# Blocks of 96 instead of 128 slots for the heavy experts of a mixture-of-experts stage on one Trainium2 core

## What is computed

```python
D_MODEL, SEQ, DEPTH = 1024, 1024, 2
N_EXPERTS, MOE_TOP_K, MOE_FF = 32, 2, 512
...
def _hier_moe(m, ...):                     # m: rmsnorm(h), 1024 tokens
    # one group of 8 experts per token, then its two best experts
    experts = g_idx * MOE_PER_GROUP + e_idx
    return _expert_dispatch(xf, experts, weights, w_gate, w_up, w_down)
...
    def expert_block(args):                # tok: the tokens of one expert e
        xb = x_pad[tok]
        hb = jax.nn.silu(xb @ w_gate[e]) * (xb @ w_up[e])
        return hb @ w_down[e]
```

## Time and profile before

| | us |
|---|---|
| median of 3 runs | 3237.29 |
| the 3 runs | 3237.29, 3222.32, 3237.57 |
| the profiled execution | 3239.65 |
| its span, first to last instruction | 3238.1 |
| mean granted TensorE clock | 0.945 of full |
| `first_blocks`, layer 0, first product to the start of the last | 852.7 to 1412.4 |
| `first_blocks`, layer 1, first product to the start of the last | 2489.7 to 3050.1 |

### The profile page before, as it was taken

One profiled execution on the slowest core, in us unless ns is written; L12 is line 12 of the kernel. 1 busy time (PEld: TensorE's weight loads), 2 busy tenths in 40 slices (PEclk: granted clock), 3 DMA queues, 4 the chain that ended last, 5 costly groups with the idle time before them and its releaser, 6 DMA issues. The chain is left out here.

```text
span 3238.1 us, 32792 instructions
## 1 busy us (share of the span) xinstructions
PE 2942.9 (91%) x12473; PEld 1583.8 (49%) x12474; DVE 1127.9 (35%) x2447; ACT 631.1 (19%) x1248; POOL 246.2 (8%) x352
## 2 busy tenths in 40 slices
PE   7999899999799999979799899577897999999798
PEld 5544555545444444434376644367654444444243
DVE  2584355544200000024371623566464000000052
ACT  3310355521100101112211111222211101101030
POOL 0000000001100000020000000134201000000110
PEclk9999899999799999989897799888997999999899
DMA  4000881031699999962110210000414999999641
GB/s 153 26 27 0 328 347 53 1 121 57 241 414 415 421 405 399 397 243 84 52 50 1 37 44 26 1 2 2 165 53 169 415 413 412 410 404 397 235 162 45
DMA packets 138550, 617.24 MB, mean 191 GB/s; under 512 B 25188, under 2 KB 31748, under 8 KB 121992
## 3 DMA queue, kind: packets, MB, share of 16 engines
q1 hardware_dynamic: 110952, 525.93, 41.2%
q0 software_dynamic: 24064, 86.00, 7.0%
q10 hardware_dynamic: 3376, 3.19, 0.3%
HBM read 508.00 MB, written 105.91 MB: 190 GB/s over the span
## 5 line engine op out<-in xcount | busy, mean ns | idle before, releaser
L1974 PE MATMUL acc<-wg,xt 128*128 128x512 f32 x512 | 222.9, 598 | 0.0
L737 PE MATMUL acc<-h,xt 128*128 128x512 f32 x384 | 165.2, 592 | 0.0
L2572 PE MATMUL acc<-xt,slabs 128*128 128x512 f32 x384 | 165.1, 592 | 0.0
L1974 PEld LDWEIGHTS acc<-wg,xt 128*128 128x128 f32 x512 | 98.5, 193 | 123.2 <-issue 123.2
L376 PE MATMUL scores<-qkt 65*128 65x512 f32 (+7 forms) x384 | 148.9, 498 | 0.9 <-DVE qkt L516 0.9
L522 DVE TENSOR_REDUCE nmax<-scores 128x1 f32<-128x256 f32 (+7 forms) x128 | 96.8, 756 | 77.5 <-PE scores L378 76.2
L1720 PE MATMUL py<-place 128*64 128x512 f32 (+1 forms) x352 | 120.2, 594 | 1.0 <-DVE place L1800 1.0
L1720 PE MATMUL pu<-place 128*128 128x512 f32 (+1 forms) x320 | 119.8, 593 | 0.0
L2572 PEld LDWEIGHTS acc<-xt,slabs 128*128 128x128 f32 x384 | 72.9, 190 | 91.4 <-issue 91.4
L737 PEld LDWEIGHTS acc<-h,xt 128*128 128x128 f32 x384 | 72.9, 190 | 91.1 <-issue 90.9
L1243 PE MATMUL acc<-place 128*128 128x512 f32 x256 | 114.3, 601 | 2.7 <-PEq L75 2.7
(11 more groups left out here) (645 smaller groups left out, 5170.1 us busy)
## 6 DMA issues: line engine op xcount, KB each, us to landing
own<-in_moe_w_gate_dram SPq DMA_DIRECT2D x22, 2048.0 KB, 16.3
place<-in_moe_w_down_dram SPq DMA_DIRECT2D x22, 2048.0 KB, 16.3
place<-in_moe_w_up_dram SPq DMA_DIRECT2D x20, 2048.0 KB, 18.2
slots_out<-zeros SPq DMA_DIRECT2D x4, 9216.0 KB, 62.8
place<-in_moe_w_gate_dram SPq DMA_DIRECT2D x18, 2048.0 KB, 21.2
own<-in_moe_w_up_dram SPq DMA_DIRECT2D x16, 2048.0 KB, 16.0
own<-in_moe_w_down_dram SPq DMA_DIRECT2D x10, 2048.0 KB, 19.5
xt<-in_moe_w_gate_dram SPq DMA_DIRECT2D x9, 2048.0 KB, 22.4
```

Source lines behind the costliest of these rows:

```text
L737: last = pe.matmul(acc[:, n % 4, 0:width], xs[:, k, tile_of(i)], weights[:, k, cols], start=(k == 0), stop=(k == k_of - 1))
L1974: last = pe.matmul(acc[:, u % 4, :], xt[:, k, i * P:(i + 1) * P], wg[:, k, n * SLAB:(n + 1) * SLAB], start=(k == 0), stop=(k == KD - 1))
L2572: last = pe.matmul(acc[:, n % 4, :], slabs[:, s % 2, k, (m % 4) * P:(m % 4 + 1) * P], xt[:, k, half * SLAB:(half + 1) * SLAB], start=(k == ...
```

## The change

The cap of a heavy expert is 96 in place of 128, in the rank table's column of caps as well. What a heavy unit moves, turns, copies and multiplies spans 96 slots: 96 rows of `xb` and `y`, 96 columns of each transpose's output, 96 stationary columns in each product. The ring, the order of the instructions, their number, the 512 moving columns of each product and the pairs are as before.

```diff
+ALONE, PAIRED = 96, 64
...
-    caps = [P if rank < HEAVY else P // 2 for rank in ranks]
+    caps = [ALONE if rank < HEAVY else PAIRED for rank in ranks]
...
-                    pool.dma_start(m[:, n, :], c.slots_in[units[n][0] * REGION:units[n][0] * REGION + P, :]).then_inc(c.x_in[n], 16)
+                    pool.dma_start(m[0:ALONE, n, :], c.slots_in[units[n][0] * REGION:units[n][0] * REGION + ALONE, :]).then_inc(c.x_in[n], 16)
...
+            def slots(n):
+                return ALONE if len(units[n]) == 1 else PAIRED
+
+            def used(n):
+                return slots(n) * len(units[n])
...
-                        last = pe.transpose(turned[:, k * P:(k + 1) * P], xb[:, n % 2].rearrange("t (p k) -> t k p", k=KD)[:, k, :], c.ident[:])
+                        last = pe.transpose(turned[:, k * P:k * P + used(n)], xb[0:used(n), n % 2].rearrange("t (p k) -> t k p", k=KD)[:, k, :], c.ident[0:used(n), 0:used(n)])
...
                 def product(n, kind, out, lhs, ks, k_last, cols):
-                    rows = P // len(units[n])
+                    rows = slots(n)
...
-                        last = pe.transpose(ph[:, k * P:(k + 1) * P], hid[:, k * P:(k + 1) * P], c.ident[:])
+                        last = pe.transpose(ph[:, k * P:k * P + used(n)], hid[0:used(n), k * P:(k + 1) * P], c.ident[0:used(n), 0:used(n)])
...
-                    act.activation(xbt[:, n % 2].rearrange("p k t -> p (k t)"), turned[:], ACT.Copy).then_inc(x_copied, 1)
+                    act.activation(xbt[:, n % 2, :, 0:used(n)], turned[:].rearrange("p (k t) -> p k t", k=KD)[:, :, 0:used(n)], ACT.Copy).then_inc(x_copied, 1)
...
-                    act.activation(y[:, n % 2, 0:SLAB], py[:, 0:SLAB], ACT.Copy).then_inc(y_act, 1)
+                    act.activation(y[0:used(n), n % 2, 0:SLAB], py[0:used(n), 0:SLAB], ACT.Copy).then_inc(y_act, 1)
...
-                    act.activation(gate, pg[:], ACT.Silu).then_inc(silued, 1)
+                    act.activation(gate[0:used(n)], pg[0:used(n)], ACT.Silu).then_inc(silued, 1)
...
-                    dve.tensor_copy(hidt.rearrange("p k t -> p (k t)"), ph[:]).then_inc(h_copied, 1)
+                    dve.tensor_copy(hidt[:, :, 0:used(n)], ph[:].rearrange("p (k t) -> p k t", k=KF)[:, :, 0:used(n)]).then_inc(h_copied, 1)
```

More of the change, by code:

```diff
@@ L1464, in _ @@
                 step(dve.tensor_scalar(cap_col[:], rank[:], float(HEAVY), None, ALU.is_lt))
-                step(dve.tensor_scalar(cap_col[:], cap_col[:], float(P // 2), float(P // 2), ALU.mult, ALU.add))
+                step(dve.tensor_scalar(cap_col[:], cap_col[:], float(ALONE - PAIRED), float(PAIRED), ALU.mult, ALU.add))
                 step(dve.tensor_tensor(over_col[:], counts, cap_col[:], ALU.subtract))
@@ L1671, in _ @@
                     if n >= RING:
-                        used, by, _ = tiles[n - RING]
-                        sp.wait_ge((gated, upped, downed)[used], (2 if used == 2 else 1) * (by + 1))
+                        before, by, _ = tiles[n - RING]
+                        sp.wait_ge((gated, upped, downed)[before], (2 if before == 2 else 1) * (by + 1))
                     sp.dma_start(ring[n % RING].rearrange("p (k n) -> p k n", k=KF if kind == 2 else KD),
@@ L1805, in y_half @@
                         dve.wait_ge(y_out[n % 2], y_before[n % 2] + 16 * arrivals[n - 2])
-                    dve.tensor_copy(y[:, n % 2, SLAB:D], py[:, SLAB:D]).then_inc(y_dve, 1)
+                    dve.tensor_copy(y[0:used(n), n % 2, SLAB:D], py[0:used(n), SLAB:D]).then_inc(y_dve, 1)
                 def results():
@@ L1838, in _ @@
                         dve.wait_ge(h_turned, n)
-                    dve.tensor_tensor(hid, gate, pu[:], ALU.mult).then_inc(hidden, 1)
+                    dve.tensor_tensor(hid[0:used(n)], gate[0:used(n)], pu[0:used(n)], ALU.mult).then_inc(hidden, 1)
                 hidden_out(UNITS - 1)
```

## The result

The changed kernel takes 3244.26 us (median of 22 runs, 3224.38 to 3249.72), the one before 3237.23 (22 runs, 3219.76 to 3239.58): a ratio of 1.0035 with a 95% interval of [1.002, 1.005]. It is 7 us slower by the medians, where 1 us faster was forecast. (The ratio says 11 us, since it is not that of the medians.) The time is inside the range given, by its upper end, but the sign is wrong, and not by chance, as the interval leaves out 1 and both layers show it. The profiled execution took 3246.25 us, with a span of 3244.7 and the same mean clock of 0.945.

What follows compares the result with a forecast made beforehand. TensorE was taken to bound the kernel, 20.6 of a heavy unit's 21.9 us being products. Terms 0 + 0 + 0.6 + 0.4 = 1.0 us less than the median 3237.29 gave 3236.3 us, range 3218 to 3246.

Steps and rivals of the forecast that it cites:

- Transfers: hidden before and after, 0: Heavy units' row loads and stores: 4.7 MB less a layer, asked for over a unit ahead, so no time gained.
- The weights wait for TensorE, not the reverse: Changed stage: TensorE has no wait for a DMA, while SP waits 168.5 us for up products to free ring tiles.
- Rival 2: DMA engines are the real bound in the stage; 9.4 MB less at 386 GB/s saves 24.4 us: 3212; chance 0.03.
- Transposes: 0, of 0 to 11.9 us: 432 transposes in heavy units keep 128 stationary columns, so 0.110 us each as before; gain 0 taken, 11.9 at most.
- Rival 1: Heavy units' transposes follow their moving columns, 128 to 96: 11.9 us more gained, 3224 us; chance 0.08.
- Products: 0.: Heavy units' products keep 512 moving columns, so 0.429 us a step with 96 stationary columns too: cost 0, gain 0.
- Rival 3: Array tiling changes at each transpose in heavy units, 0.6 us a unit, 22 us slower: 3258; chance 0.03.
- Rivals 4 and 5: 4: experts over 96 tokens bring overflow blocks, 3276, chance 0.01. 5: tiles still filled to 128, time as now.
- Loads laid bare beside a pair, -0.6: Stationary loads that cannot run ahead beside pairs: 0.075 for 0.10 us at 24 places, 0.6 us gained.
- copies, -0.4: ACT's copy falls to 0.81 us, on the path only at each stage's first gate: 0.2 us a layer, 0.4 gained.

Runs made afterwards that it cites:

- e2: The kernel before with only 96 rows of a heavy unit loaded and stored, compute still on 128 slots: 3243.83 us, ratio 1.0014 to before.
- s1: The changed kernel with 128 rows loaded, 96 stored, and only 2 of the 8 steps of every up product: 3221.21 us, one run.
- t1: As e4, but the 8 transposes `turned` take stationary columns that are neighbours in SBUF, with other results: 3224.86 us, one run.
- e1: The changed kernel with 128 rows of a heavy unit loaded and stored, compute on 96: 3228.42 us, ratio 0.9975 to before.
- s10: As s1, but the 128 rows of a heavy unit come in two loads of 96 and 32 rows: 3260.46 us, one run.
- e4: The changed kernel with 128 rows of a heavy unit loaded and 96 stored, compute on 96: 3229.63 us, ratio 0.9967 to before.

## Why the prediction was wrong

**"Transfers: hidden before and after, 0" is the step that failed.** It asked whether the rows of a unit arrive in time, and they do: TensorE never waited for them. It did not ask what their transfer does to the weights'. The term measures +5.8 / +6.2 us a stage, 12.0 us, in place of 0 (9.9 us by e2 against before), and its sign is the opposite of what 9.4 MB less suggest.

**The margin of the weights was misread.** "The weights wait for TensorE, not the reverse" was true of before, but it is a statement of sign and not of size. SP's waits only say that a ring tile was not free yet; they stayed at 161.5 us while the weights became late. The size of the margin was in sight: a DMA share of 1.01 in the earlier trace rows leaves little slack, and the demand, 401 GB/s of 408, works out from the earlier trace rows and the tiles' 2 MB, a margin of 2%. The earlier trace rows gave 386 GB/s in one window of 50 us, taken for what the engines do. One such window is too short for that: in s1, where TensorE waits for weights throughout, the same window has 374 GB/s and the whole stretch 407. From 900 to 1350 us before did 408.

**Rival 2, the DMA engines as the real bound, was right in its mechanism and wrong in its sign.** It was priced by bytes at a fixed rate, 24 us faster, chance 0.03. The rate was what changed. No rival had a smaller transfer that makes the others slower, though "transfers" was the one edit costed at nothing while its resource was full.

**Transposes: 0, of 0 to 11.9 us.** Between. `ph` follows its moving columns (0.083, the other end), 72 of them in a layer; `turned` hardly moves (0.107). The earlier trace rows showed that a full stationary load takes 0.106 where little moves; they do not bound a transpose of 96, as `ph` and t1's `turned` at 0.083 show. The gain is 0.13 us a unit, 2.3 us a stage, 4.6 in all. Rival 1 was right for a third of the transposes, and a term put at 0 was worth 4.6 us.

**Products: 0.** Right: 0.429 us a step with 96 stationary columns. **Rival 3**, a change of tiling: 21.80 us a unit in place of 22.5, so 96 columns count as 128 do. **Rivals 4 and 5** did not come about: no block over the cap, and rows of 96 in every form.

**Loads laid bare beside a pair, -0.6, and copies, -0.4.** Both about right. Three heavy units and a pair take 0.46 us less than before (22.57, 22.52, 22.04 and 21.93 us became 22.44, 22.46, 21.90 and 21.80), of which 0.39 are the transposes. That leaves 0.07 for the loads laid bare, where 0.05 was forecast. The copy took its 0.81 us, and the first gate's wait went from 1.11 us to 0.9.

The sum by the steps as measured: -5.7 for the narrower compute (e1 against before) and +12.0 for the transfers (after against e1) are +6.3 us. That they add up to the stages' difference is so by the way they are taken and proves nothing; e2 and before give +9.9 for the transfers on their own, and with it +4.2. The sign is the same, for 7.0 us between the medians. The prediction had named as its own test a stage off by over 5 us with unit periods as now, "for then I have missed what bounds its ends"; each stage is off by 3, with periods shorter than now, and what was missed does act at the end.

## What to carry to other kernels

"Engine X never waits" is not a margin. Where the DMA engines' share stands at 1, work out what the stage wants per second and what it gets, and follow the time from issue to landing along the stage: here a queue that shrinks (23.4, 16.2, 15.0 us) against one that doesn't (27.6, 31.1, 29.8) shows the loss by 1250 us, over 100 us before TensorE first waits for a tile. Beside heavy traffic, a smaller load may not be a cheaper one: cut the compute to what is in use, store what is in use, and keep row loads at 128 rows in one transfer unless a run says otherwise.

## What was unexpected in the hardware

- A load of fewer than 128 rows, or of 128 in two pieces, issued by POOL, lowers the rate of all DMA traffic meanwhile: from 407 or 408 GB/s to 392 (96 rows), 389 (112), 386 (120), 390 (64 + 32), 386 (96 + 32), 382 (64 + 64), by s1 to s10. A store of 96 rows does not (407 and 410, e4 and e1).
- A transpose of float32 with 128 stationary and 96 moving columns takes 0.083 us where the stationary columns are neighbours and 0.107 where they lie 32 bytes apart; with 128 moving columns it takes 0.108 and 0.111 (`ph` and `turned` of the earlier trace rows), so there the layout matters little.
- When the weights' queue is long, issuing itself takes time. SP's load instructions mostly take 0.33 us. In before one took 5.7 us at 852 us, after five others within 3 us, and none over 1.2 us late in the stage; in after they took up to 8.7 us there (duration in ns, min/median/max, 1300 to 1400 us):
```profile
L1681 SPq DMA_DIRECT2D place<-in_moe_w_up_dram x4: 333/1488/8706, 1327.0 to 1373.6; - x4
```
